# Product with w_o taken by parts of the inner dimension on its first two token tiles, and the low parts of the merged branches made between the branch products

## What is computed

```
y = (sigmoid(gA) * A + sigmoid(gB) * B) @ w_o          # A: attention branch, B: convolution branch
h = layer_norm(alpha * x + y)
g_logits = h @ w_rg + b_rg ;  e_logits = h @ w_re + b_re
g_sel = argmax(g_logits) ; top 2 of the 8 experts of that group
out = layer_norm(alpha * h + moe(h))                     # 32 SwiGLU experts, each 1024 -> 512 -> 1024
```

## Time and profile before

| what | value |
|---|---|
| median of 3 runs | 1245.51 us (1243.91 to 1245.95) |
| profiled execution, its own time | 1245.54 us |
| profiled execution, span (first to last instruction) | 1243.5 us |
| PE busy | 1146.5 us (92% of the span) |
| PE weight loads busy | 908.5 us (73%) |
| DVE, ACT, POOL busy | 827.3, 575.2, 268.1 us |
| mean granted TensorE clock | 0.943 of full speed |

### The profile page before, as it was taken

How to read it: one execution, slowest core, us unless ns; L and a number is a source line. 1 busy time by engine, 2 the same in 40 slices (tenths; PEclk the granted TensorE clock), 3 DMA queues, 4 the chain that set the end, 5 groups by cost and what they waited for, 6 DMA issues and landing times.

```text
span 1243.5 us, 16070 instructions
## 1 busy us (share of the span) xinstructions
PE 1146.5 (92%) x5990; PEld 908.5 (73%) x5990; DVE 827.3 (67%) x945; ACT 575.2 (46%) x524; POOL 268.1 (22%) x185
## 2 busy tenths in 40 slices
PE   6999999979899999799589999999999999999980
PEld 5999998868688778676457777777777777777760
DVE  1089999500401573633669998888888888889856
ACT  2322211111301236100347877787787778777850
POOL 2344520000000002400112233223322332332110
PEclk9999999989867999898689999999999999999995
DMA  6468632145130064021669999999999999999823
GB/s 250 160 245 310 243 145 82 46 170 188 48 102 34 13 259 140 1 102 71 281 207 358 371 371 368 355 359 348 374 361 352 360 361 361 359 359 376 318 76 145
DMA packets 40336, 293.06 MB, mean 236 GB/s; under 512 B 10927, under 2 KB 14639, under 8 KB 24557
## 3 DMA queue, kind: packets, MB, share of 16 engines
q1 hardware_dynamic: 26029, 262.53, 55.7%
q0 software_dynamic: 10720, 25.98, 7.0%
q10 hardware_dynamic: 3552, 4.06, 1.0%
HBM read 286.83 MB, written 41.12 MB: 264 GB/s over the span
## 4 chain that ended last, share of the span: by engine, by line
PE 86%; DVE 5%; DMA 3%; issue 2%; POOL 2%; ACT 1%; SPq 1%; POOLq 0%; ACTq 0%; DVEq 0%
PE ps L580 9%; PE ps L870 9%; PE ps L872 9%; PE ps L871 9%; PE ps L894 5%; PE ps L896 5%; PE ps L895 5%; PE ps L542 3%; PE ps L544 3%; PE ps L543 3%; PE ps L712 2%; PE ps L788 2%; PE ps L853 2%; PE ps L818 2%; PE ps L820 2%
## 5 line engine op out<-in xcount | busy, mean ns | idle before, releaser
L1549 DVE TENSOR_TENSOR region_b_split<-region_b,z_split 128x2048 fp32r<-128x2048 f32 x96 | 216.9, 2286 | 26.1 <-ACT z_split L1103 25.5
L1549 DVE TENSOR_TENSOR region_a_split<-region_a,z_split 128x2048 fp32r<-128x2048 f32 x96 | 216.7, 2285 | 23.2 <-ACT z_split L1103 23.1
L870 PE MATMUL ps<-z_split,scratch_split 128*96 128x512 f32 x512 | 206.6, 404 | 1.9 <-DVE scratch_split L1554 1.9
L872 PE MATMUL ps<-z_split,scratch_split 128*96 128x512 f32 x512 | 202.0, 395 | 0.0
L1103 ACT CAST z_split<-region_a 128x2048 fp32r<-128x2048 f32 x96 | 179.9, 1909 | 0.0
L1103 ACT CAST z_split<-region_b 128x2048 fp32r<-128x2048 f32 x94 | 176.1, 1908 | 2.0 <-PE ps L872 2.0
L580 PE MATMUL ps<-x_columns,region_b 128*128 128x272 f32 x512 | 142.2, 429 | 9.0 <-DMA region_b<-in_w_in_pairs 9.0
L1242 DVE SCALAR_TENSOR_TENSOR z_conv_gates<-scratch,column_vectors,z_conv_gates 128x512 f32<-128x512 f32 (+1 forms) x240 | 133.9, 630 | 0.0
L580 PEld LDWEIGHTS ps<-x_columns,region_b 128*128 128x128 f32 x512 | 102.5, 207 | 30.1 <-DMA region_b<-in_w_in_pairs 9.1
L542 PE MATMUL ps<-z_split,region_b_split 128*128 128x272 f32 x384 | 111.1, 289 | 3.5 <-POOL region_b_split L1652 3.5
L544 PE MATMUL ps<-z_split,region_b_split 128*128 128x272 f32 x384 | 111.2, 290 | 0.0
(11 more groups left out here) (264 smaller groups left out, 1804.2 us busy)
## 6 DMA issues: line engine op xcount, KB each, us to landing
region_b<-in_w_expert_gate SPq DMA_DIRECT2D x16, 2048.0 KB, 11.9
region_a<-in_w_expert_up SPq DMA_DIRECT2D x16, 2048.0 KB, 11.9
region_a<-in_w_expert_gate SPq DMA_DIRECT2D x16, 2048.0 KB, 11.7
region_a<-in_w_expert_down SPq DMA_DIRECT2D x16, 2048.0 KB, 11.5
region_b<-in_w_expert_up SPq DMA_DIRECT2D x16, 2048.0 KB, 12.4
region_b<-in_w_expert_down SPq DMA_DIRECT2D x16, 2048.0 KB, 11.5
region_b<-in_w_in_pairs SPq DMA_DIRECT2D x21, 1024.0 KB, 4.8
region_b<-in_cache_tiles POOLq DMA_DIRECT2D x16, 768.0 KB, 4.6
```

The source lines that it names most:

```text
L870: pe.matmul(out, xh[:, k, :], hi[:, k, :], start=k == 0, stop=False)
L872: last = pe.matmul(out, xl[:, k, :], hi[:, k, :], start=False, stop=k == KD - 1)
L1549: ve.tensor_tensor(low_part[place][:, part], raw[place][:, part], high_part[high or w][:, part].bitcast(F32), ALU.subtract).then_inc(low_s ...
```

## The change

The wait for all of `x_split` ahead of the product goes. PE waits for the seventh part of the branches to be read (`br_used`, 7: banks 0 to 3 are then free) and takes the first two token tiles together, by parts k of the inner dimension: for k = 0 to 5 it waits for that part of `ga_lo` (and each second time for a quarter of `wo_lo`) and makes 12 matmuls, 3 for each of the four banks; parts 6 and 7 follow for tile 0 and then for tile 1. Tiles 2 to 4 are as before. `router(0)` comes after tile 2, right ahead of `router(1)`, and was after tile 1. DVE makes part m-2 of `ga_lo` after branch part m, from m = 2 on, and the last two at the end. ACT takes the square roots of tiles 0 and 1 ahead of the first copy of turned rows, and DVE adds the router's bias one tile later. The number of instructions of each kind stays the same.

```diff
--- before.py
+++ after.py
@@ -790,12 +790,10 @@
                         last = pe.matmul(ps[:, s + 2 + half, 0:HALF], wa[:, k, m * P:(m + 1) * P], at[:, k, cols], start=k == 0, stop=k == 1)
                 last.then_inc(br_ps, 1)
 
-            pe.wait_ge(w_split, SPLIT + 4)
-            pe.wait_ge(x_split, 2 + KD)
-            pe.wait_ge(wr_loaded, 32)
-
             def router(t):
                 c0, n = TILES[t]
+                if t == 0:
+                    pe.wait_ge(wr_loaded, 32)
                 pe.wait_ge(hdone, t + 1)
                 if t >= 1:
                     pe.wait_ge(ht_sb, t)
@@ -809,18 +807,35 @@
                     last = pe.matmul(ps[0:n, 6 + t % 2, 0:36], hcol[:, k, 0:n], wrv[:, k, :], start=k == 0, stop=k == KD - 1)
                 last.then_inc(lg_ps, 1)
 
-            for t, (c0, n) in enumerate(TILES):
-                if t >= 2:
-                    pe.wait_ge(y_used, t - 1)
+            def rows_out(t, ks):
+
+                c0, n = TILES[t]
                 for half in range(2):
                     out, cols = ps[0:n, 2 * (t % 2) + half, :], slice(half * 512, (half + 1) * 512)
-                    for k in range(KD):
+                    for k in ks:
                         pe.matmul(out, ga_hi[:, k, c0:c0 + n], wo_hi[:, k, cols], start=k == 0, stop=False)
                         pe.matmul(out, ga_hi[:, k, c0:c0 + n], wo_lo[:, k, cols], start=False, stop=False)
                         last = pe.matmul(out, ga_lo[:, k, c0:c0 + n], wo_hi[:, k, cols], start=False, stop=k == KD - 1)
-                last.then_inc(y_ps, 1)
-                if t >= 1:
-                    router(t - 1)
+                return last
+
+
+            pe.wait_ge(br_used, KD - 1)
+            for k in range(KD - 2):
+                if k % 2 == 0:
+                    pe.wait_ge(w_split, SPLIT + k // 2 + 1)
+                pe.wait_ge(x_split, 2 + k + 1)
+                for t in range(2):
+                    rows_out(t, [k])
+            pe.wait_ge(w_split, SPLIT + 4)
+            pe.wait_ge(x_split, 2 + KD)
+            for t in range(2):
+                rows_out(t, range(KD - 2, KD)).then_inc(y_ps, 1)
+            for t in range(2, NTT):
+                pe.wait_ge(y_used, t - 1)
+                rows_out(t, range(KD)).then_inc(y_ps, 1)
+                if t == 2:
+                    router(0)
+                router(t - 1)
             router(NTT - 1)
 
             pe.wait_ge(mset, 1)
@@ -1087,10 +1102,17 @@
                     ac.wait_ge(lg_ps, t)
                 ac.copy(hcol[:, :, 0:n1], ps[:, 4:6, :].rearrange("p b (k c) -> p (b k) c", k=4)[:, :, 0:n1]).then_inc(ht_sb, 1)
 
-            for t, (c0, n) in enumerate(TILES):
-                s = t % 2
+            def root(t):
+                n = TILES[t][1]
                 ac.wait_ge(hvar, t + 1)
-                ac.activation(sd[s][0:n], var_e[s][0:n], ACT.Sqrt).then_inc(hsd, 1)
+                ac.activation(sd[t % 2][0:n], var_e[t % 2][0:n], ACT.Sqrt).then_inc(hsd, 1)
+
+            root(0)
+            root(1)
+            columns_out(0)
+            columns_out(1)
+            for t in range(2, NTT):
+                root(t)
                 columns_out(t)
 
             def split_high(w, e, c, place, rounds, done):
@@ -1367,6 +1389,10 @@
                     work[kind](i)
             columns(3)
 
+            def merged_low(m):
+                ve.wait_ge(x_high, 2 + m + 1)
+                ve.tensor_tensor(ga_lo[:, m, :], ga[:, m, :], ga_hi[:, m, :].bitcast(F32), ALU.subtract).then_inc(x_split, 1)
+
             for m in range(KD):
                 s = 4 * (m % 2)
                 ve.wait_ge(gate_sig, m + 1)
@@ -1379,10 +1405,10 @@
                     ve.wait_ge(w_high, SPLIT + j + 1)
                     two = slice(2 * j, 2 * j + 2)
                     ve.tensor_tensor(wo_lo[:, two, :], wo[:, two, :], wo_hi[:, two, :].bitcast(F32), ALU.subtract).then_inc(w_split, 1)
-
-            for m in range(KD):
-                ve.wait_ge(x_high, 2 + m + 1)
-                ve.tensor_tensor(ga_lo[:, m, :], ga[:, m, :], ga_hi[:, m, :].bitcast(F32), ALU.subtract).then_inc(x_split, 1)
+                if m >= 2:
+                    merged_low(m - 2)
+            merged_low(KD - 2)
+            merged_low(KD - 1)
 
             def statistics(rows, s, n, done, eps):
 
@@ -1398,6 +1424,12 @@
             link(ve.tensor_scalar(io32, iota_e.unsqueeze(1).broadcast_to(S32), -64.0, None, ALU.add))
             ve.wait_ge(rows1_loaded, 32)
             ve.wait_ge(br_loaded, 32)
+
+            def logits_out(t):
+                n = TILES[t][1]
+                ve.wait_ge(lg_ps, t + 1)
+                ve.tensor_tensor(lg[0:n, t, :], ps[0:n, 6 + t % 2, 0:36], br[0:n], ALU.add).then_inc(lg_sb, 1)
+
             for t, (c0, n) in enumerate(TILES):
                 s = t % 2
                 ve.wait_ge(y_ps, t + 1)
@@ -1414,12 +1446,10 @@
                 ve.wait_ge(hsd, t + 1)
                 link(ve.reciprocal(rs[s][0:n], sd[s][0:n]))
                 ve.scalar_tensor_tensor(hs, hs, rs[s][0:n], b1row[0:n], ALU.mult, ALU.add).then_inc(hdone, 1)
-                if t >= 1:
-                    c1, n1 = TILES[t - 1]
-                    ve.wait_ge(lg_ps, t)
-                    ve.tensor_tensor(lg[0:n1, t - 1, :], ps[0:n1, 6 + (t - 1) % 2, 0:36], br[0:n1], ALU.add).then_inc(lg_sb, 1)
-            ve.wait_ge(lg_ps, NTT)
-            ve.tensor_tensor(lg[0:NS, 4, :], ps[0:NS, 6, 0:36], br[0:NS], ALU.add).then_inc(lg_sb, 1)
+                if t >= 2:
+                    logits_out(t - 2)
+            logits_out(NTT - 2)
+            logits_out(NTT - 1)
             ve.wait_ge(lg_sb, NTT)
 
 
```

## The result

| | before | changed |
|---|---|---|
| median of 4 runs beside each other | 1245.73 us (1243.91 to 1246.73) | 1233.46 us (1230.71 to 1235.52) |
| ratio | | 0.9902, 95% interval 0.9874 to 0.9929 |
| profiled execution, its own time | 1245.54 us | 1235.37 us |
| span | 1243.5 us | 1233.4 us |
| mean granted clock | 0.943 | 0.946 |

The change makes the kernel 12.3 us faster in the medians and 10.2 us in the profiled executions. The chain that ended last, around the branches and up to the reading of the last token tile. One line of before comes first: the start of the branch products, which stands nowhere above.

What follows compares the result with a forecast made beforehand. PE sets the pace, waiting 7.83 us for the eighth low part. Tiles 0 and 1 end 9.9 us earlier, tile 2 gains 1.4, router 1 loses 1.4: 1245.54 - 9.9 = 1235.6 us, range 1232.6 to 1239.5.

Steps and rivals of the forecast that it cites:

- The pause: Between the last branch product and the product with w_o: the 7.83 us go, at most some tenths stay.
- The first two tiles at 0.232 us a step: Tiles 0 and 1 of the product: 96 matmuls at full clock in 22.3 us, 2.1 us less than before.
- DVE between the branches: Branch parts from m = 3: DVE needs 4.3 or 5.5 us against PE's 5.50; 4 us of slack, cost zero.
- POOL might wait 0.7 us more: POOL's sum between the branches may wait 0.7 us more for DVE; its reader is two parts away, cost zero.
- The last low part: End of ga_lo: all eight parts there by about 520.5, PE reaches part 6 at 532.1; slack 11 us, hidden.
- The order of banks: Tiles 0 and 1, another bank after every third matmul: cost zero, as in the expert's down product.
- The rule that the prediction weighed: The 96 matmuls: going around the banks starves the clock, 41.3 us at 1.2 GHz, 1254.6 us in all; rival, 4%.
- Tile 2 right behind: Tile 2 after tiles 0 and 1: no wait, margin 1.4 us; 11.1 us at full clock, 1.4 us gained.
- The routers: Routers 0 and 1 together behind tile 2: router 0 4.2 us, router 1 1.4 more at half clock, bounds 0 and 2.9.
- tile 3's spell: Tile 3 behind router 1: half-clock start left as before, 12.78 us; could be 1.6 us less or 1.8 more.
- the bound of 12.9: Upper bound of the gain, 1232.6 us: router 1 costs nothing and tile 3's spell vanishes.
- Carried to the end: Behind tile 4: everything hangs on tile 4, so the 9.9 us gain reaches the end, 1235.6 us.

Runs made afterwards that it cites:

- e6: The changed kernel with PE waiting for all parts of ga_lo and wo_lo ahead of the product; 1242.6 us, 0.9976 of before.
- e7: The changed kernel with eight idle DVE subtractions ahead of the last ga_lo part; 1234.5 us, 0.9902 of before.
- e4: The kernel before with tiles 0 and 1 taken by parts, still waiting for all low parts, routers as before; 1252.8 us, 1.0070 of before.
- e2: The changed kernel with router 0 after tile 1 again, ACT's and DVE's order as before; 1241.0 us, 0.9965 of before.
- e5: The changed kernel run again, unchanged, with its profile; 1236.8 us, 0.9914 of before.
- e8: The changed kernel with each router split, transposes between the halves of a later tile and products behind that tile; 1227.0 us, 0.9851 of before.
- e10: The changed kernel with all eight ga_lo subtractions after the branches again, second run of this edit; 1240.4 us, 0.9949 of before.

## Why the prediction was right

1235.6 us was forecast with 1232.6 to 1239.5; 1233.46 was measured. By the steps:

- **The pause.** 7.83 us gone, with nothing in its place, as forecast. e6 brings it back by its wait alone, and e7 shows the slack behind it: 10 us later costs nothing.
- **The first two tiles at 0.232 us a step.** Right: 22.3 us, granted clock 1.00.
- **DVE between the branches.** 4.3 or 5.5 us a part had been left open; with the subtraction at 1.86 in all four it was 5.3 to 5.9 from one line 1400 to the next, and that line began at most 0.5 us behind PE. The slack of 4 us was hardly touched. That POOL might wait 0.7 us more was wrong: POOL took the same 3.31 us and DVE waited. The last low part was forecast 5.1 us after the branches and came after 4.8. The Trainium skill, "SBUF — State Buffer", section "Who interferes with whom", has a DVE instruction with two SBUF inputs and a POOL instruction that reads SBUF take turns, each holding the shared pair to its end. The trace agrees: the 1.86 us from 516.76 are 0.71 us of work and 1.15 of waiting, which end about where POOL's sum does (514.72 + 3.31 = 518.03).
- **The order of banks.** Cost zero, by the down product's rows; e4 shows it with this product's own. The rule that the prediction weighed, of the Trainium skill, "TensorE: Matmul & The Clock Gate", section "A second HAM failure mode: psum-queue depth-cycling", is about a kernel in which TensorE idles between its groups. That does not come up here: in e4's stretch PE is busy for 18.00 of 18.00 us and the clock stays at 1.00.
- **Tile 2 right behind.** Right: 33.4 us for three tiles, no wait.
- **The routers.** This is the term that was mis-sized, in both directions. Router 1 at half clock was put at 1.4 us as a middle, because its products seemed too short to scale with the clock. They scale: 3.63 against 1.98 us, and transposes of 1.95 against 0.89 (e2), so a router wholly at 1.2 GHz costs 2.7 us more, near the bound that was named (2.9). In e5 half of that came (1.65), and tile 3's spell of 1.5 where 1.6 had been kept; e5's stage is 10.0 us shorter than before's, and 9.9 was the forecast. But in two of three profiles the clock did not fall at routers 0 and 1 or in tile 3, and the stage won 13.1 and 13.2 us, just outside the bound of 12.9. Router 1 then took 3.98 us, where the prediction named 5 to 6 us at half clock as a sign; only e5 has it (5.6). The sum took the spell for certain, because it had come at every router before, and in no profile of the changed kernel did router 1 begin at half clock, as the sum had it: in e5 its transposes still took 0.92 us.
- **Carried to the end.** Right: 645.9 and 645.6 us behind the stage.

The number for the profiled execution (1235.37 against 1235.6) came out so near with some luck: 3.1 us more were won at the routers than summed, and 3.3 us were lost in the attention part, which the change does not touch. The median, 2.1 us below the forecast, lies inside the range.

## What to carry to other kernels

When an engine waits for the last of several operands that arrive one by one, look at what it could do with the first. Here the order of the loops (the inner dimension outside, over two output tiles and four banks) bought 22 us of matmuls during which the rest could arrive, and it cost nothing in itself. But such an order finishes its tiles together, late and close to each other, so whatever was placed between them (here router 0) now waits for the work on the first one's result (here the norm of tile 0). It has to move behind the next tile, or much of the gain goes there: 7.5 us of 12.3 in e2. In e4, which has the order without the early start, the kernel ends 7.6 us above before. A chain that goes over another engine and back gained here by being cut in two, with independent matmuls between the halves: a further 9.8 us in the medians (e8).

## What the runs showed of the hardware

Small operations of TensorE, transposes of 128 columns and products of 36, follow the granted clock nearly in full: 0.89 to 1.95 us for eight transposes, 1.98 to 3.63 us for a router's products.

Whether the clock falls at a stretch of short, interrupted work differs between executions of the same kernel: at routers 0 and 1 it fell in one profile of three, worth 3.1 us of 1235. A pause of 2.3 us did not lower it at once (e10); behind pauses of 3.3, 4.88 and 7.83 us it stood at 0.50 (e2, e6, before). The length of one pause does not decide it alone: in the kernel before it fell at router 0 too (0.50 at 551.5), where TensorE's longest wait was 1.1 us.
